# A hybrid attention step on one core: scoring two units ahead of the exponential, in the same PSUM banks

## What is computed

```python
def swa_attend(q, k, v, q_pos, k_pos, mk, mv, sinks, slopes):     # branch 0
    s = jnp.einsum('bqkgd,bskd->bkgqs', qg, k).astype(jnp.float32)
    ...
    s = jnp.where(ok, s - slopes[None, :, :, None, None] * dist, -jnp.inf)
    p = jax.nn.softmax(jnp.concatenate([s, sm, sink], axis=-1), axis=-1).astype(v.dtype)
    ...
def dsa_attend(q, qi, wi, q_pos, k, v, ki, mk, mv, slopes, n_sel):  # branch 1
    top_val, top_idx = lax.top_k(score, n_sel)
    ...
    s = jnp.where(valid[:, None, None], s - slopes[None, :, :, None, None] * dist[:, None, None], -jnp.inf)
    p = jax.nn.softmax(jnp.concatenate([s, sm], axis=-1), axis=-1).astype(v.dtype)
    out = (jnp.einsum('bkgqn,bqnkd->bqkgd', p[..., :n_sel], v_sel)
           + jnp.einsum('bkgqm,bmkd->bqkgd', p[..., n_sel:], mv))
```

## Time and profile before

| | |
|---|---|
| median of 3 runs | 2042.55 us (2040.95 to 2051.41) |
| the profiled execution | 2042.43 us, span 2040.6 us |
| PE matmul busy | 1924.3 us, 94% of the span |
| DVE busy | 1178.2 us, 58% |
| ACT busy | 713.2 us, 35% |
| POOL busy | 578.8 us, 28% |
| mean granted clock of TensorE | 0.964 |

### The profile page before, as it was taken

How to read it: one execution, slowest core, us unless ns; L and a number is a source line. 1 busy time by engine, 2 the same in 40 slices (tenths; PEclk the granted TensorE clock), 3 DMA queues, 4 the chain that set the end, 5 groups by cost and what they waited for, 6 DMA issues and landing times. The chain is left out here.

```text
span 2040.6 us, 31131 instructions
## 1 busy us (share of the span) xinstructions
PE 1924.3 (94%) x11132; PEld 1734.4 (85%) x11132; DVE 1178.2 (58%) x2701; ACT 713.2 (35%) x1421; POOL 578.8 (28%) x444
## 2 busy tenths in 40 slices
PE   5989999999849999999997989999999999999995
PEld 5879999877638999999996868888888888888884
DVE  5249999998746566666754653333333333333337
ACT  4335544233215555655544332112122121212122
POOL 2315554133213232445611002222222222222224
PEclk9999999999977999999978999999999999999998
DMA  5423333332349134444613312111111111111104
GB/s 166 130 71 85 93 95 88 94 106 80 81 92 185 39 70 89 95 92 93 122 38 115 138 57 93 42 41 41 41 46 41 42 45 41 46 41 46 54 8 154
DMA packets 147465, 160.18 MB, mean 78 GB/s; under 512 B 35776, under 2 KB 115504, under 8 KB 147360
## 3 DMA queue, kind: packets, MB, share of 16 engines
q1 hardware_dynamic: 136416, 141.10, 26.0%
q10 hardware_dynamic: 10944, 17.72, 3.7%
HBM read 120.63 MB, written 39.27 MB: 78 GB/s over the span
## 5 line engine op out<-in xcount | busy, mean ns | idle before, releaser
L2042 PE MATMUL ps<-x2T_hi,weights 128*128 128x362 f32 (+1 forms) x1536 | 383.8, 329 | 5.3 <-DVE weights L2008 5.3
L2060 PE MATMUL ps<-weights,hid_hi 128*128 128x512 f32 (+1 forms) x1152 | 363.0, 396 | 0.0
L2042 PEld LDWEIGHTS ps<-x2T_hi,weights 128*128 128x128 f32 x1536 | 273.9, 189 | 7.0 <-DVE weights L2008 5.5
L1993 DVE TENSOR_TENSOR total<-total,ps 128x512 f32<-128x512 f32 (+1 forms) x270 | 184.9, 687 | 164.2 <-PE ps L2060 163.3
L2060 PEld LDWEIGHTS ps<-weights,hid_hi 128*128 128x128 f32 (+1 forms) x1152 | 209.6, 182 | 57.1
L2042 PE MATMUL ps<-x2T_lo,weights 128*128 128x362 f32 (+1 forms) x768 | 253.1, 330 | 0.0
L1978 DVE TENSOR_TENSOR hidden<-hidden 128x362 f32<-128x362 f32 (+1 forms) x96 | 51.6, 537 | 311.6 <-ACT hidden L1951 311.6
L2060 PE MATMUL ps<-weights,hid_lo 128*128 128x512 f32 (+1 forms) x576 | 228.1, 396 | 0.0
L869 DVE MATCH_REPLACE8 score<-top,score 128x1024 f32<-128x1024 f32 (+6 forms) x224 | 207.2, 930 | 0.0
L865 DVE MAX8 top<-score 128x8 f32<-128x1024 f32 (+6 forms) x224 | 203.1, 937 | 1.9
L1911 POOL TENSOR_TENSOR weights<-down_raw,weights 128x512 fp32r<-128x512 f32 x64 | 83.0, 1296 | 419.6 <-ACT weights L1942 419.6
(11 more groups left out here) (188 smaller groups left out, 3618.6 us busy)
## 6 DMA issues: line engine op xcount, KB each, us to landing
w_raw<-in_w_in ACTq DMA_DIRECT2D x64, 256.0 KB, 3.0
up_raw<-in_w_up SPq DMA_DIRECT2D x64, 256.0 KB, 2.8
down_raw<-in_w_down SPq DMA_DIRECT2D x64, 256.0 KB, 2.6
q_raw<-q_scr SPq DMA_DIRECT2D x30, 512.0 KB, 8.1
gates<-gate_scr SPq DMA_DIRECT2D x34, 256.0 KB, 4.7
x_in<-in_x_prompt SPq DMA_DIRECT2D x16, 512.0 KB, 4.7
gate_scr<-stage SPq DMA_DIRECT2D x32, 256.0 KB, 3.1
q_scr<-stage SPq DMA_DIRECT2D x40, 181.0 KB, 3.0
```

The source lines that it names most:

```text
L1993: dve.tensor_tensor(out, out, ps[:r, UP_BANKS + g % DOWN_BANKS, :], ALU.add).then_inc(added, 1)
L2042: last = pe.matmul(ps[:, g % UP_BANKS, 0:n], a[:, k, fs], b, start=(k == 0 and i == 0), stop=(k == KT - 1 and i == 2))
L2060: last = pe.matmul(ps[:r, UP_BANKS + g % DOWN_BANKS, :], a, b[:, f, cols], start=(f == 0 and i == 0), stop=(f == FT - 1 and i == 2))
```

## The change

PE scores unit 1 ahead of its loop too, and in step u it scores unit u + 2 instead of u + 1. So the score of a unit stands one step earlier in PE's queue, and the turning and weighing stand where they stood. Banks, buffers, semaphores and the loops of the other engines are as before.

```diff
--- before.py
+++ after.py
@@ -1536,11 +1536,12 @@
                     last.then_inc(valued, 1)
 
                 score(0)
+                score(1)
                 for u in range(STEPS):
                     if u >= 2 and u - 2 < UNITS:
                         turn(u - 2)
-                    if u + 1 < UNITS:
-                        score(u + 1)
+                    if u + 2 < UNITS:
+                        score(u + 2)
                     if u >= 3 and u - 3 < UNITS:
                         weigh_values(u - 3)
```

## The result

| | before | after |
|---|---|---|
| median of the runs, us | 2046.98 (4 runs, 2040.95 to 2051.59) | 2170.91 (4 runs, 2169.38 to 2174.74) |
| ratio | | 1.061 [1.0571, 1.0649] |
| profiled execution, us | 2042.43, span 2040.6 | 2174.74, span 2173.0 |
| mean granted clock of PE | 0.964 | 0.934 |

What follows compares the result with a forecast made beforehand. PE was taken to set the pace, itself waiting about 1 us. Waits of 53.0 + 18.2 + 13.3 - 0.6 = 83.9 us on 2042.4 gave 2126; 32 us of low clock made 2158, range 2110 to 2200.

Steps and rivals of the forecast that it cites:

- The rival of a hidden wait: Second chunk of two-chunk units: waits hidden anyway, so not slower, 2041.5 us; chance 0.03 for no change.
- that of a shorter chain: DVE frees banks sooner: two-chunk waits go, three-chunk ones stay; 2073 us, between 2053 and 2110; chance 0.07.
- The 5.0 us among the signs of the prediction: Block 14: steps were expected to last 4.1 and 5.0 us in turn in the profile after.
- The alternation of odd and even by DVE's copy: Two-chunk blocks: even turned units wait 0.64 us; odd ones 0.35 to 0.60 us more, DVE copying before subtracting.
- waits in tile 7 (blocks 14 and 15): PE's new waits for banks in seven units of block 14 and in block 15, 25.1 us; block 15 alone 18.2.
- waits in tile 8 (block 16): Sample tile: four steps as in block 15, 8.9 us, and three short steps, 4.4 us more; 13.3 in all.
- less 0.6 for the first turn: Start of attention: the third score fills the first turn's wait for the exponential, gaining 0.6 us.
- clock in tile 7: Six of block 15's eight steps at the low clock, 3.4 us more each: 20.2 us.
- clock in the narrow section behind it: Tile 6's 16 narrow steps entered low and staying low, 0.76 us more each: 12.2 us.
- the upper case: All of block 15 and four steps of block 16 low as well: 2126 + 27 + 12 + 13 = 2178 us.
- the cases of 0.33 and 0.52: Waits alone, clock as before, 2112 to 2140 us, chance 0.33; waits with low stretches, 2141 to 2200, chance 0.52.
- Some 80 us of PE waiting: Sign expected at L1504: PE waits for DVE's neg and neg_part, some 80 us in total instead of 1 us.

Runs made afterwards that it cites:

- e1: Kernel after, but units with two or three score chunks, and the one behind each, scored one ahead as before: 2043.24 us, ratio 0.9984 to the kernel before.
- e3: Kernel after with score(k+2) put behind weigh_values(k-3) instead of ahead of it: 2076.61 us, ratio 1.013 to the kernel before.
- e5: Kernel after with a fourth probs buffer and one pt buffer less (3): 2137.89 us, ratio 1.0439 to the kernel before.
- e7: Kernel after with four probs buffers, three pt buffers and all copies of turned groups on ACT: 2063.76 us, ratio 1.0074 to the kernel before.
- e2: Kernel after, but three-chunk units (blocks 15 and 16) and the unit behind them scored one ahead as before: 2103.73 us, ratio 1.0272 to the kernel before.
- e4: Kernel after with extra matmuls, results never read, filling PE's waits for banks: 2134.0 us, ratio 1.0396 to the kernel before.
- e6: Kernel after with all copies of turned groups on ACT, three probs buffers kept: 2152.1 us, ratio 1.0424 to the kernel before.
- e9: Kernel before with 115 useless matmuls of 128 columns at the end of the projection stage: 2052.72 us, ratio 1.0015.
- e12: Kernel before with 118 useless matmuls ending the projection stage and 9 more ahead of the first score: 2042.55 us against 2050.24, ratio 0.9977.

## Why the prediction was right, and where it was off

**Direction and cause: right.** The forecast was 2158 us, 116 over the profiled execution of before; the profiled execution of the kernel after took 2174.74, 132 over it. Without new work, scoring two ahead asks for a bank whose release depends on the turn directly ahead in PE's queue. e1 shows that only units of more than one chunk pay, e3 that the order behind the turn decides, e5 to e7 that both ties which the prediction named (the subtraction to the turn by probs, and the copy in DVE's in-order queue) are real and act together. The rival of a hidden wait is excluded by the 0.98 and 0.38 us in block 14, that of a shorter chain by e2's 60 waits, in the count and size that were worked out.

**Steps.** In block 14 the working gives 3.49 + 1.24 = 4.73 and 3.49 + 0.64 = 4.13 us; measured are 4.75 and 4.14. (The 5.0 us among the signs of the prediction doesn't follow from that working.) In block 15 it gives 6.40; e4, with the clock held, shows 6.22. A step of it at the low clock was to cost 3.4 us more; it cost 9.44 - 6.22 = 3.22. The alternation of odd and even by DVE's copy came as described, and vanished in e6.

**The terms of the sum**, forecast beside measured. The waits are e4's excess over before, read from the starts of the turns (L1518) of eight units each and added by tile; the clock is the excess of the kernel after over e4.

| term | forecast, us | measured, us |
|---|---|---|
| waits in tile 7 (blocks 14 and 15) | 25.1 | 24.6 |
| waits in tiles 6, 5, 4, 3 | 14.1, 13.4, 12.7, 5.9 | 13.6, 12.7, 11.7, 6.0 |
| waits in tile 8 (block 16) | 13.3 | 13.6 |
| waits in all (tiles 2 and 1: -0.2) | 84.5, less 0.6 for the first turn | 82.1 |
| clock in tile 7 | 20.2 | 24.8, of which block 15 has 23.1 |
| clock in the narrow section behind it | 12.2 | 0 |
| clock in block 13 | 0 | 13.1 |
| clock in tile 8 (block 16) | 0 in the point, 12 in the upper case | 13.5 |
| clock in all | 32.4 | 51.4 |

e4's own low stretch in tile 0 is the longer form, 9.4 us more, and is left out of both terms; there the kernels before and after are alike. The sum of the measured terms is 133.5, beside 132.4 between the spans of the two profiled executions. That is no test of the split, since e4 cancels in the sum; what bears it out is that e4 and the kernel after agree where both are at 1.00.

**What was mis-sized: the clock.** The prediction put the fall in the right place, and it is a fall that the waits cause (e4). Two things were wrong in it. The narrow section behind block 15 was not entered low: the clock rose at 748 us, just ahead of its first turn (749.68), and its steps take what they took in the earlier trace rows, high:

```profile
753.26 0.39 PE L1518 MATMUL ps<-ident,probs 128*128 128x128 f32 x2
...
754.10 0.39 PE L1518 MATMUL ps<-ident,probs 128*128 128x128 f32 x2
```

That is 0.84 us a step. In e6, where the clock was still low at that point, the section did stay low, so it was the time of the rise that the prediction had wrong. And the clock fell again where I had not put it: 809 to 840 us, in block 13, and in block 16. The forecast had the latter only in its upper case. Why block 13 falls in the kernel after and not in e2, which has the same two-chunk waits there, the runs don't tell; the difference between them is what PE did in block 15 some 60 us earlier. (e5 has yet another fall among two-chunk units, 3.4 us in block 11, from 863.8 us on.) Part of the closeness of 2158 is luck: the 12.2 us of a narrow section that did not come stood in for some of the 26.6 us of blocks 13 and 16 that did. A small slip besides: the range holds the cases of 0.33 and 0.52, which make 0.85 and not 0.83.

The Trainium skill, in "TensorE: Matmul & The Clock Gate", section "A second HAM failure mode: psum-queue depth-cycling", has the clock go up and down in a kernel that pauses briefly between its groups. The traces agree: 0.50, 1.00, 0.51, 1.00 over the four stretches from 683 us on, with pauses of 0.2 to 1.3 us, and 1.00 in e4, where the pauses are filled.

**Some 80 us of PE waiting: right in the sum, differently booked.** The waits of PE have 50.6 + 1.2 us, those of its weight loads 78.6 + 6.0. In the low stretches a wait is shorter, because the turn ahead of it takes longer beside the same DVE; with a held clock (e2) 60 waits have 35.4 us on PE and 54.1 on the weight loads.

## What to carry to other kernels

Before an in-order engine is sent further ahead, ask of every wait that this brings what releases it, and whether that in turn hangs on the instruction directly ahead in the same queue: then each step costs a whole round trip (here turn, copy, subtraction). Count the banks against the chunks in flight, not against the units. A wait on TensorE costs more than its length once the clock falls: measure the wait and the clock apart, by filling the waits with work that nobody reads.

## What the runs showed of the hardware

Short pauses were enough to halve the clock. With block 15's scores PE was idle for 0.2 to 1.3 us at a time, 1.70 us in the step whose rows stand above (667.63 to 673.69 us), and its clock went to 0.50 for 65 us; the two-chunk steps alone, with 0.38 and 0.98 us in 4.1 and 4.8, held 1.00 for 416 us in the profiled execution of e2.

Filling these pauses with 500 useless matmuls (seven of them in a row took 1.06 us) made the kernel 37 us faster. With a pause of 4.92 us the clock fell after 24 us of unbroken matmuls (e9); with one of 2.98 us at the same place it did not (e12). None of this explains the fall in tile 0, at 1018.6 us before and 1123 after: PE was busy 31.00 of 31 us in both stretches, and in the kernel before 28.28 of the 28.6 us ahead of the fall. It is in every trace here, with 31 to 65 us, and is open.
